# Moving the sides of the down projection to GpSimd and two high halves per pair round to ScalarE in a streaming-encoder trunk

## The reference, cut to what matters

```python
def conv_ffn(x, w_up, conv_w, conv_b, w_down):
    hdn = x @ w_up
    hdn = causal_dwconv(hdn, conv_w, conv_b)
    val, gate = jnp.split(hdn, [D_FF], axis=-1)
    return (jax.nn.gelu(gate) * val) @ w_down
...
    log_a = -LRU_C * r.astype(jnp.float32) * jax.nn.softplus(-lam.astype(jnp.float32))
```

## Time and profile before

| | |
|---|---|
| median of 3 runs | 1247.02 us (1246.19 to 1247.81) |
| profiled execution's own time | 1246.39 us |
| its span, first to last instruction | 1244.7 us |
| mean granted TensorE clock | 0.995 |
| PE busy | 1222.8 us, 98% |
| DVE busy | 870.1 us, 70% |
| ACT busy | 505.4 us, 41% |
| POOL busy | 699.8 us, 56% |

### The profile page before, as it was taken

The page is one execution under the profiler, slowest core; times in us unless marked ns, Lnnn a source line. Parts: engine busy times, 40 slices in busy tenths (PEclk is TensorE's granted clock), DMA queues, the critical chain, the costliest instruction groups (busy, mean ns, idle before and its releaser), DMA issues.

```text
span 1244.7 us, 17985 instructions
## 1 busy us (share of the span) xinstructions
PE 1222.8 (98%) x6165; PEld 1011.6 (81%) x6165; DVE 870.1 (70%) x1220; ACT 505.4 (41%) x835; POOL 699.8 (56%) x798
## 2 busy tenths in 40 slices
PE   9999999999999997999999999999999999999998
PEld 6887777788888985877888778888889888888887
DVE  6555556588878778799844365287887877899842
ACT  4445444223444421564144286113344433564141
POOL 7554467729767695200177556847876789200173
PEclk9999999999999998999999999999999999999999
DMA  5212132303132242676143222322223234576221
GB/s 199 70 68 68 68 118 88 116 1 101 69 122 80 103 146 90 192 215 201 68 153 118 85 68 85 118 68 68 90 80 106 97 118 151 190 218 202 68 94 60
DMA packets 74204, 137.54 MB, mean 111 GB/s; under 512 B 4272, under 2 KB 52976, under 8 KB 73632
## 3 DMA queue, kind: packets, MB, share of 16 engines
q1 hardware_dynamic: 73088, 134.23, 32.8%
q10 hardware_dynamic: 1056, 2.58, 0.6%
HBM read 134.60 MB, written 2.20 MB: 110 GB/s over the span
## 4 chain that ended last, share of the span: by engine, by line
PE 74%; DVE 16%; DVEq 5%; ACT 2%; issue 2%; DMA 1%; ACTq 0%; SPq 0%
PE bank L607 12%; PE bank L609 12%; PE bank L608 12%; PE bank L626 4%; PE bank L628 4%; PE bank L627 4%; PE bank L959 3%; PE bank L963 3%; PE bank L961 3%; DVE w_lo L1585 3%; DVE tmp L1412 2%; PE bank L903 2%; PE bank L901 2%; DVEq L1411 2%; PE bank L722 1%
## 5 line engine op out<-in xcount | busy, mean ns | idle before, releaser
L593 POOL TENSOR_TENSOR w_lo<-stage,w_hi 128x256 fp32r<-128x256 f32 x528 | 413.3, 813 | 82.4 <-DVE w_lo L1492 62.6
L585 POOL TENSOR_SCALAR w_hi<-stage 128x1024 fp32r<-128x1024 f32 x132 | 157.5, 1193 | 302.0 <-PE bank L628 168.7
L607 PE MATMUL bank<-x_hi,w_hi 128*128 128x512 f32 (+1 forms) x520 | 202.5, 389 | 9.2 <-DVEq L1416 9.2
L608 PE MATMUL bank<-x_lo,w_hi 128*128 128x512 f32 (+1 forms) x520 | 201.8, 388 | 0.0
L609 PE MATMUL bank<-x_hi,w_lo 128*128 128x512 f32 (+1 forms) x520 | 201.5, 387 | 0.0
L607 PE MATMUL bank<-in_hi,w_hi 128*128 128x512 f32 x312 | 130.0, 417 | 0.0
L1960 ACT ACTIVATE tmp<-bank,cols 128x512 f32<-128x512 f32 x88 | 63.7, 774 | 147.3 <-PE bank L609 111.3
L607 PEld LDWEIGHTS bank<-x_hi,w_hi 128*128 128x128 f32 x520 | 98.3, 189 | 29.9 <-issue 9.2
L609 PE MATMUL bank<-in_hi,w_lo 128*128 128x512 f32 x312 | 122.1, 391 | 0.0
L608 PE MATMUL bank<-in_lo,w_hi 128*128 128x512 f32 x312 | 122.0, 391 | 0.0
L609 PEld LDWEIGHTS bank<-x_hi,w_lo 128*128 128x128 f32 x520 | 98.2, 189 | 20.1
(11 more groups left out here) (255 smaller groups left out, 2835.6 us busy)
## 6 DMA issues: line engine op xcount, KB each, us to landing
stage<-w_square SPq DMA_DIRECT2D x163, 512.0 KB, 3.3
stage<-w_down SPq DMA_DIRECT2D x52, 512.0 KB, 3.8
stage_far<-w_down SPq DMA_DIRECT2D x24, 512.0 KB, 4.8
rows<-norm_rows SPq DMA_DIRECT2D x4, 1024.0 KB, 5.9
outT<-x SPq DMA_DIRECT2D x7, 256.0 KB, 2.0
x<-xT SPq DMA_DIRECT2D x3, 512.0 KB, 6.6
p_in<-pT ACTq DMA_DIRECT2D x2, 512.0 KB, 5.6
w_ai<-w_lru SPq DMA_DIRECT2D x1, 1024.0 KB, 8.4
```

Source lines behind the costliest of these rows:

```text
L585: whole = pool.tensor_scalar(high[:, s, :], stage[:, s, :], 1.0, 0.0, ALU.mult, ALU.add)
L593: piece = pool.tensor_tensor(low[:, s, to], stage[:, s, to], high[:, s, to].bitcast(F32), ALU.subtract)
L607: pe.matmul(out, w_hi[:, s, c:c + P], m_hi, start=first, stop=False)
L608: pe.matmul(out, w_hi[:, s, c:c + P], m_lo, start=False, stop=False)
```

## The change: three edits

**Sides.** `SIDES_AT` is gone. POOL makes the sides of groups 0 to 5 (`early_side`), one group inside each `pair_released`, that is in each of rounds 3 to 8 before the last low piece of unit 0. DVE keeps groups 6 and 7, after rounds 8 and 9, with a counter of its own.

**High halves.** In rounds 3 to 8 the high halves of the ordinary units 0 and 1 are written by ACT (`plain_top`), in the round before: unit 0 of round i+1 after `pair_keep(i, 2)`, unit 1 after `pair_keep(i, 3)`. POOL waits for them (`plain_high`) in place of writing them, and still writes the four low pieces.

**Decay rates.** `decay_magnitudes`, ACT's exponential and `decay_rates` are taken out of layer 0's up phase and stand between layer 0's second layer norm and its embedding gate.

```diff
-SIDES_AT = {3: (0,), 5: (1,), 7: (2, 3), 8: (4, 5), 9: (6, 7)}
+LATE_SIDES = {8: (6,), 9: (7,)}
...
+            def early_side(layer, n):
+
+                side = folded[:, n, :, :]
+                pool.wait_ge(h_ready, layer * FT + 2 + 2 * (n + 1))
+                pool.tensor_tensor(side[:, 1, :], side[:, 0, :], side[:, 6, :], ALU.subtract)
+                pool.tensor_tensor(side[:, 3, :], side[:, 6, :], side[:, 5, :], ALU.subtract)
+                pool.drain()
+                pool.tensor_tensor(side[:, 4, :], side[:, 3, :], side[:, 0, :], ALU.subtract)
+                pool.drain()
+                pool.tensor_tensor(side[:, 6, :], side[:, 4, :], side[:, 2, :], ALU.add)
+                pool.drain()
+                pool.sem_inc(fold_sides_ready, 1)
+
             def pair_released(layer, i):
 
+                early_side(layer, i - PAIR_FIRST)
                 pool.wait_ge(pair_low, (layer * UP_PAIRS + i - PAIR_FIRST + 1) * 4)
                 pool.sem_inc(unit_split, 2)
...
-                        whole = pool.tensor_scalar(high[:, s, :], stage[:, s, :], 1.0, 0.0, ALU.mult, ALU.add)
+                        if is_up and PAIR_FIRST < i <= PAIR_END and r < 2:
+                            pool.wait_ge(plain_high, (int(name[-1]) * UP_PAIRS + i - PAIR_FIRST - 1) * 2 + r + 1)
+                        else:
+                            whole = pool.tensor_scalar(high[:, s, :], stage[:, s, :], 1.0, 0.0, ALU.mult, ALU.add)
...
-                    for n in SIDES_AT.get(i, ()):
+                    for n in LATE_SIDES.get(i, ()):
                         fold_sides(n)
...
-                    if layer == 0 and i == 4:
-                        decay_magnitudes()
-                    if layer == 0 and i == 8:
-                        decay_rates()
...
                 layer_norm(2 * layer + 1, layer)
+                if layer == 0:
+                    decay_magnitudes()
+                    decay_rates()
                 gate(layer)
...
+            def plain_top(layer, i, r):
+
+                ph = phases[f"up{layer}"]
+                s = ph.slots[r] % SLOTS
+                act.wait_ge(unit_loaded[s], ph.fills(i, r) * 16)
+                act.wait_ge(unit_used, ph.slot_free(i, r))
+                act.copy(w_hi[:, s, :], stage[:, s, :]).then_inc(plain_high, 1)
...
                         pair_keep(layer, i, 2)
+                        plain_top(layer, i + 1, 0)
                         pair_keep(layer, i, 3)
+                        plain_top(layer, i + 1, 1)
                         conv_own(layer, i, 1)
```

More of the change, by code:

```diff
@@ L306, in hybrid_trunk_kernel @@
             sem(n) for n in ("fold_summed", "fold_high", "side_high", "side_ready"))
-        fold_sides_ready, first_summed, fold_low = (
-            sem(n) for n in ("fold_sides_ready", "first_summed", "fold_low"))
+        fold_sides_ready, late_sides_ready, first_summed, fold_low = (
+            sem(n) for n in ("fold_sides_ready", "late_sides_ready", "first_summed", "fold_low"))
         product_done, bank_kept, bank_folded = (
@@ L313, in hybrid_trunk_kernel @@
         pair_product, pair_kept, pair_joined = (sem(n) for n in ("pair_product", "pair_kept", "pair_joined"))
+        plain_high = sem("plain_high")
         unit_split = sem("unit_split")
@@ L1447, in fold_sides @@
                 dve.drain()
-                dve.sem_inc(fold_sides_ready, 1)
+                dve.sem_inc(late_sides_ready, 1)
             def half_sums(n):
@@ L1981, in side_top @@
                                 phases[f"up{layer}"].done(FT // 2 - 1, 3))
-                act.wait_ge(fold_sides_ready, layer * PRE + step % PRE + 1)
+                if step % PRE < UP_PAIRS:
+                    act.wait_ge(fold_sides_ready, layer * UP_PAIRS + step % PRE + 1)
+                else:
+                    act.wait_ge(late_sides_ready, layer * (PRE - UP_PAIRS) + step % PRE - UP_PAIRS + 1)
                 act.copy(high_of(step), side_of(folded, step)).then_inc(side_high, 1)
@@ L2035, in conv_ffn @@
                         side_top(layer, PRE)
-                    if layer == 0 and i == 5:
-                        act.wait_ge(lam_abs, 1)
-                        act.activation(lam4[:, 1, :], lam4[:, 1, :], ACT.Exp, scale=-1.0).then_inc(lam_exp, 1)
                 for i in range(PRE):
@@ L2146, in rest_of_layer @@
                 layer_norm_out(2 * layer + 1, layer)
+                if layer == 0:
+                    act.wait_ge(lam_abs, 1)
+                    act.activation(lam4[:, 1, :], lam4[:, 1, :], ACT.Exp, scale=-1.0).then_inc(lam_exp, 1)
                 gate(layer)
```

## The result

The change is slower. Its median is 1298.37 us (1298.19 to 1299.06) against 1247.38 us before, a ratio of 1.0411 with a 95% interval of 1.0393 to 1.0429: 51 us. The forecast was 1275 us with a range of 1266 to 1295 us, so the direction was right and the size was not. The profiled execution took 1298.26 us, 51.9 us more than that of before.

The account below looks back on a forecast made before the run. The prediction took PE to bound the kernel (busy 1222.8 of 1244.7 us). 1246.39 us less 15.7 removed plus 43.8 of new waits gave 1274.5 us profiled, 1275 us as median with 0.6 added; range 1266 to 1295 us.

Parts of the forecast that it names:

- PE bounds the kernel: Whole kernel: PE sets the time, being busy for 1222.8 of 1244.7 us at nearly full clock.
- What the edits remove: Up phase: four pair waits (4.5 us), one wait of 8.75 us and its low-clock tail (2.5 us) go, 15.7 us.
- Decay rates at the gate: Layer 0's gate: the moved chain costs zero, given DVE's idle 10.36 us and 6.2 us of cover behind ACT's copy.
- The chain from P4: Rounds 3 to 8, both layers: after P4, ACT's high half and POOL's work make PE wait 3.65 us, 12 times, 43.8 us.
- The pair's start: Pair rounds: later loads and POOL sums still arrive before PE needs them for P3, with 2.9 us of cover; nothing added.
- The clock, at zero in the sum: Behind the 12 new PE waits: the sum included no time for a lower clock.
- rival (a): The clock falls behind new waits: 2.5 us each, 30 us for all 12, 1305 us; some to all, chance 0.12.
- the prediction's own signs of being wrong: New PE wait under 1.5 us, clock falling behind the new waits, or another wait at P1 or P3.
- The faster outcome: Rounds 3 to 8: the new order hides behind P5 to P7, only removed waits count, 1231 us; chance 0.06.
- The pair that starts late: Pair rounds: loads or POOL's sums overrun 2.9 us of cover; one us past it each round gives 1287 us; chance 0.06.

Follow-up runs that it names:

- the fillers: The changed kernel plus 14 unused matmuls by PE ahead of unit 0 in rounds 3 to 8, inside its wait for POOL: 1275.53 us, ratio 1.0234.
- the early high halves: The changed kernel with ACT's two high halves moved forward, behind keep 0 and keep 1 of the pair: 1243.66 us, ratio 0.9968.
- 7 fillers: The changed kernel plus 7 unused matmuls by PE ahead of unit 0 in rounds 3 to 8: 1285.60 us, ratio 1.0299.
- half a side: The changed kernel with two of the side's four instructions before unit 0's last low piece and two behind unit 1: 1263.63 us, ratio 1.0125.

## Why the prediction was wrong in size and right in place

**PE bounds the kernel.** Right. In the six kernels whose clock stayed at 1.00, PE's busy time less that of the fillers is 1220.0 to 1224.2 us. What moved the time beyond these 4 us was PE's standing still or its clock.

**What the edits remove, 15.7 us.** Right. The change with POOL's high halves gains 15.3 us, the one with unit 1's high half by ACT 15.2 us, the one with the side behind unit 1 13.2 us. The tail of 2.5 us belongs in it: the decay rates alone gain 12.4 us, more than the wait.

**Decay rates at the gate, nothing.** Right, with the reason of the forecast. DVE's timeline after, its last instruction of the rates and the gate's first product:

```profile
663.12 0.17 DVE L1679 TENSOR_SCALAR lam<-lam 128x8 f32<-128x8 f32 x1
666.99 0.70 DVE L1700 TENSOR_TENSOR bank<-bank,emb 128x512 f32<-128x512 f32 x1 [3.70 <-ACT bank L2122]
```

The chain takes 3.9 us beside an idle POOL (659.42 to 663.29 us) and not the 10 us that it took in the up phase, and 3.70 us of DVE's idle time are left.

**The chain from P4, 3.65 us a round, 43.8 us.** Right: 3.58 us a round, 42.9 us. Each link held: the high half 1.05 us, three pieces 2.13, the side 3.15 with its drains up to the last instruction's end, the last piece 0.72. The choice of 0.71 us between the bounds of 0.65 and 0.84 us was right for this place, since in it DVE reads banks. Where POOL runs beside DVE's work in SBUF, as with the early high halves, 0.84 or more would have been the price.

**The pair's start, covered.** Right. No wait at P1 or P3 is in the list of PE's waits.

**The clock, at zero in the sum.** This is the step that failed. The prediction had the mechanism as rival (a), priced at 2.5 us a tail and 1305 us for twelve, but gave it 0.12 and kept it out of the sum, on the argument that waits of 1.3 us had left the clock alone, that the wait of 8.75 us had not, and that 3.65 us "lies between the two". The fillers show that the missing 23 us are this, to within about 2 us, and the clock that falls behind the new waits was among the prediction's own signs of being wrong. The price was right to within 0.3 us (2.2 us measured). The chance was wrong: of waits of 3.4 to 3.9 us 22 of 24 had a tail (two kernels), of 1.8 to 2.0 us 7 of 12 (with 7 fillers), of 1.7 to 1.8 us 5 of 12 (half a side), and of 1.4 us or less none. Where two rows lie on either side and the price multiplies by twelve, a half would have been the fairer chance, and it would have put the range's upper end at rival (a)'s 1305 us.

**The rivals on the other side.** The faster outcome, 1231 us, did not come, but its number is that of each kernel in which the chain is broken: 1230.4, 1230.8 and 1232.9 us. The pair that starts late played no part.

What stays open is when exactly the clock falls. Equal waits of 1.84 us in one kernel ended with and without a tail, and no run here separates what decides it.

## What to carry to other kernels

When work is handed from one engine to another, first ask what the new engine is waiting for at that point of its stream: ACT was 41% busy and POOL idle for 8.5 to 10.2 us a round, and both facts were beside the point, because ACT's instruction stood behind a wait for P4 and POOL's whole chain stood behind it. Two edits that are each nearly free can share one cover; count their chains together, from the latest event that starts them to the instruction that PE waits for. And price a wait of PE with the lower clock behind it as soon as it is longer than those for which the trace shows the clock to stay.

The best versions are the change without unit 0's high half on ACT (1230.4 us, ratio 0.9875) and the one that leaves both high halves with POOL (1230.8 us, ratio 0.9873); these runs don't tell them apart.

## What the runs showed of the hardware that was not expected

PE's granted clock can fall after waits as short as 1.8 us, and then not after each of them. It can fall after PE has resumed: for the wait that ended at 356.58 us the clock was 1.00 for the next us and 0.50 from about 357.8 us on. So a short wait can cost more than its length: waits of 2.0 us with PE busy for 1.6 us before them cost 8 us over twelve rounds more than waits of 0.45 us that ended at the same point.

A matmul that computes nothing can pay for itself. 14 fillers a round, written into a bank that is about to be overwritten, made the changed kernel 23 us faster, 1275.5 for 1298.4 us, although they removed no dependency. It is still slower than the kernel before, 1246.1 us on the same chip.
